# Half-tile instead of quarter-tile pieces of the mixing projections, between the steps of attention and delta rule, with another tile order

## The chip, the cores and the metric

One core of a Trainium2 chip runs the whole layer in one program. The metric is the device time of one execution in microseconds (us). The kernel before takes 1328.13 us, the median of 3 runs (1328.02 to 1328.16).

## The reference, cut to what matters

One decoder layer over 512 positions of width 1024, in fp32. The mixing half computes three branches from one normalised input `n`:

```python
n = rms_norm(h, ln_mix_pre)
da_q, da_k, da_v, dn_q, dn_k, dn_v, dn_z, dn_b, dn_a, ca_q, gate_logits = split(n @ w_in)
y_a = diff_attention(da_q, da_k, da_v, ...)        # 8 heads, two softmax maps a head
qkv = short_conv(concat(dn_q, dn_k, dn_v), conv_w) # causal, width 4, silu
o_dn = gated_delta_rule(cq, ck, cv, g, beta)       # 8 heads, chunks, a triangular solve in each
y_b = rms_norm(o_dn, dn_norm_g) * silu(dn_z)
mk, mv = split(rms_norm(mem, mem_norm_g) @ w_mem_kv)
y_c = memory_attention(ca_q, mk, mv)               # 4 heads, 256 memory tokens
proj = einsum('bsiw,iwd->bsid', stack(y_a, y_b, y_c), w_branch)
mixed = sum(sigmoid(gate_logits) * proj)
h = h + rms_norm(mixed @ w_out, ln_mix_post)
f = square(relu(rms_norm(h, ln_ff_pre) @ w_ff1)) @ w_ff2
h = h + rms_norm(f, ln_ff_post)
```

## The kernel before, in words

Every large product is cut into weight tiles of 1024 rows by 128 columns. A tile of weights is loaded by a DMA on SyncE's queue into `w_raw` (three buffers), split by ScalarE into a rounded part `w_hi` (L1105, "hi") and by VectorE into the rest `w_lo` (L1407, "lo"; three slots), and TensorE multiplies it in 8 slices of 128 rows, three products to a slice: `n_hi` by `w_hi` (L1906), `n_lo` by `w_hi` (L1907), `n_hi` by `w_lo` (L1908). Such a tile is 24 multiplications of 512 columns into one of two banks of `acc`; ScalarE empties the bank ("evac") before the tile after the next may begin.

The mixing stage has 104 such tiles: `dq`, `dk`, `dv`, `dz` for the delta rule, `aq`, `ak`, `av` for the differential attention, `mk`, `mv`, `cq` for the memory attention (`mk` and `mv` over 256 columns), and 24 `gate` tiles. Between pieces of these tiles stand the 178 steps of the two other chains of work: `attn` (for a memory head cs, ct, cv; for a head av, as0, as1, at, ap, ay) and `delta` (for each of 4 pairs of heads dk, dE, dq, dv, dL, T1, dA, the solve Za, Wb, Z5, W5, Zl, Wl, then dU, dW, the chunks sa, sb, and dO). A step is a few short products or transposes on TensorE (into `ps_a` or `ps_d`), whose result is worked on by ScalarE, VectorE or GpSimd before the next step of its chain may start. The names in the profile: `d_XB` is what Za leaves and Wb reads, `sums_lo` is what dE reads, `o_a` what ay reads.

The order of all this is fixed before the program is built. `ORDER` is a table of tile kinds; `mixing_tiles` makes the sequence of tiles of it. `plan_order` then places the work of each engine: it gives each piece a length and the pieces that it needs (a table `parts` says how a tile is divided for TensorE), and lets each engine take, of the families that are ready, the first in a list of ranks; on TensorE a step that is ready goes ahead of the next piece of a tile. Every engine then runs its list strictly in order, and waits on semaphores.

What follows the mixing stage is the branch stage: 24 tiles `br` multiply the branches' outputs by `w_branch`, first the 8 of the memory attention. Its first tile waits for each slice `k` of the branch apart:

```python
if r % KT == 0:
    k_wait = lambda k, b=b: pe.wait_ge(yl_ready, KT * b + k + 1)
```

The branch outputs were stored to HBM by their steps (`y_scratch`), since SBUF has no room for them. The eight slices of the first branch are read back in the family "pre": SyncE loads slice kk into `y_st[kk % 2]` (L977; from kk = 2 on when the slice two before is done with its buffer, `yl_ready` at kk - 1), VectorE rounds it to `y_hi` (L1684), GpSimd makes the rest `y_lo` (L1070) and counts `yl_ready`. These three stand in the engines' fixed lists too, between the last steps of the mixing stage. dO of the last pair (L2053) is transposed on TensorE, multiplied on VectorE by `zs` into `d_ET` (L1675), and stored by SyncE (L968); `zs` comes of the last two tiles, `dz6` and `dz7`, by ScalarE (`z_t`, L1201) and VectorE (L1544), one after the other.

Of the kernel before, what the change touches and what calls it, by code (L numbers as in the profile page):

```python
# [86 lines left out]


ORDER = [("first", 0), ("z", 0), ("mem", 0), ("cq", 0), ("cq", 1), ("cq", 2), ("cq", 3), ("conv", 1), ("head", 0),
         ("head", 1), ("gate", 1), ("conv", 2), ("head", 2), ("gate", 2), ("head", 3), ("z", 1), ("gate", 1),  # L90
         ("head", 4), ("gate", 2), ("z", 2), ("head", 5), ("conv", 3), ("head", 6), ("gate", 2), ("head", 7),
         ("gate", 13), ("z", 3)]

# [112 lines left out]
def plan_order(tiles, need_free, n_first):  # L208
# [5 lines left out]
    n_mix = len(tiles)  # L214
    conv = [t for t in range(n_mix) if tiles[t][0] in ("dq", "dk", "dv")]
    zt = [t for t in range(n_mix) if tiles[t][0] == "dz"]
    gate = [t for t in range(n_mix) if tiles[t][0] == "gate"]
    spill = [i for i, s in enumerate(attn) if s[0] in ("cv", "ay")]
    short = lambda t: tiles[t][0] in ("mk", "mv")
    finished = lambda t: tiles[t][0] in ("dq", "dk", "dv", "dz")  # L220
    parts = {t: ((0, 4), (4, 8)) if short(t) else ((0, 2), (2, 4), (4, 6), (6, 8)) for t in range(n_mix)}
    last = {t: ("PE", "main", t) + parts[t][-1] for t in range(n_mix)}
    busy, needs, queue = {}, {}, {}

# [162 lines left out]
def plan_tiles():  # L387

    tiles, need_free = mixing_tiles()
    n_mix = len(tiles)  # L390
    order, planned = first_order(tiles), plan_order(tiles, need_free, FIRST)
    for e in order:
        order[e] += planned[e]
    tiles = list(tiles)
    for i in (2, 0, 1):
        tiles += [("br", i * KT + m) for m in range(KT)]
    tiles += [("out", m) for m in range(KT)]
    for half in range(2):
        tiles += [("f1", half * 16 + f) for f in range(16)]
        tiles += [("f2", (2 * half + g) * KT + m) for g in range(2) for m in range(KT)]  # L400
    return tiles, n_mix, order, need_free
# [1989 lines left out]
```

## Time and profile before

| what | us |
|---|---|
| median of 3 runs | 1328.13 (1328.02 to 1328.16) |
| the profiled execution, its time | 1327.76 |
| its span, from the first to the last instruction | 1326.0 |
| TensorE busy in it | 1307.4 (99%) |
| VectorE, ScalarE, GpSimd busy | 758.0, 461.7, 187.6 |
| mixing stage, tiles with steps between them | about 77 to 788.5 of the span |
| first tile of the branch stage on TensorE | starts at 788.53 |

The share of busy time names the bound (TensorE), but its ends are modelled, so a busy engine may still lose some tenths of a microsecond at each change of work. Two things are read from the trace instead: the list of what TensorE waited for, and the distance from one matmul's start to the next one's. Matmuls of 512 columns that follow each other start every 0.23 us, so a larger distance is a loss at that place.

### The profile page before, as it was taken

The numbers are of one execution on the slowest core, as the hardware profiler recorded it, in microseconds if no ns is written. First come the engines' busy times: TensorE is split into PE (matmuls) and PEld (weight loads), VectorE is DVE, ScalarE is ACT, GpSimd is POOL, SyncE is SP. The second block draws the span as 40 slices with busy tenths as digits, with TensorE's granted clock in tenths as the row PEclk, the third lists the DMA queues.
The fourth block names the chain that finished last, engine by engine and source line by source line (L and its number), as shares of the span: only waits on it lengthen the run. The fifth ranks groups of instructions, "written<-read, shape, count | busy, mean of one in ns | idle before, by whom it ended". The sixth has DMA issues, their size and how long they took to land.

```text
span 1326.0 us, 23795 instructions
## 1 busy us (share of the span) xinstructions
PE 1307.4 (99%) x10193; PEld 1092.5 (82%) x10193; DVE 758.0 (57%) x1278; ACT 461.7 (35%) x765; POOL 187.6 (14%) x128
## 2 busy tenths in 40 slices
PE   9999999999999999999999999999999999999997
PEld 8879988787788887888878888888888888888886
DVE  6786335576576576577965354555576522355335
ACT  5343433444353444343534331112433212222220
POOL 1023000013000023000331412233012200022000
PEclk9999999999999999999999999999999999999999
DMA  5155413221212232212223537653504333323321
GB/s 218 60 177 171 129 48 111 80 84 62 81 65 80 82 101 90 64 58 101 83 89 97 161 111 231 209 162 130 220 33 127 95 113 98 91 96 98 108 64 64
DMA packets 62832, 144.03 MB, mean 109 GB/s; under 512 B 5072, under 2 KB 28168, under 8 KB 62728
## 3 DMA queue, kind: packets, MB, share of 16 engines
q1 hardware_dynamic: 62728, 142.51, 33.2%
q8 instruction: 81, 1.33, 0.4%
q14 instruction: 23, 0.19, 0.1%
HBM read 127.79 MB, written 16.27 MB: 109 GB/s over the span
## 4 chain that ended last, share of the span: by engine, by line
PE 89%; DVE 6%; issue 2%; ACT 1%; DMA 1%; POOL 0%; SPq 0%; DVEq 0%; ACTq 0%; POOLq 0%
PE acc L1906 17%; PE acc L1908 16%; PE acc L1907 16%; PE ps_a L1907 2%; PE ps_a L1906 2%; PE ps_a L1908 2%; PE ps_a L2015 2%; PE ps_d L2093 2%; PE ps_d L2223 2%; PE ps_a L2223 2%; PE ps_d L2224 2%; PE ps_a L2225 2%; PE ps_a L2224 2%; PE ps_d L2225 2%; DVE w_lo L1407 1%
## 5 line engine op out<-in xcount | busy, mean ns | idle before, releaser
L1407 DVE TENSOR_TENSOR w_lo<-w_raw,w_hi 128x1024 fp32r<-128x1024 f32 x170 | 233.0, 1371 | 208.2 <-ACT w_hi L1105 207.5
L1105 ACT CAST w_hi<-w_raw 128x1024 fp32r<-128x1024 f32 x170 | 178.1, 1048 | 406.5 <-PE acc L1908 331.6
L1906 PE MATMUL acc<-n_hi,w_hi 128*128 128x512 f32 x744 | 303.3, 408 | 1.2 <-ACT conv_x L1180 1.2
L1908 PE MATMUL acc<-n_hi,w_lo 128*128 128x512 f32 x744 | 290.7, 391 | 0.0
L1907 PE MATMUL acc<-n_lo,w_hi 128*128 128x512 f32 x744 | 290.2, 390 | 0.0
L1906 PEld LDWEIGHTS acc<-n_hi,w_hi 128*128 128x128 f32 x744 | 139.9, 188 | 30.8 <-issue 3.8
L1908 PEld LDWEIGHTS acc<-n_hi,w_lo 128*128 128x128 f32 x744 | 139.6, 188 | 30.3
L1907 PEld LDWEIGHTS acc<-n_lo,w_hi 128*128 128x128 f32 x744 | 140.1, 188 | 25.8 <-issue 0.7
L1093 POOL TENSOR_TENSOR h_lo<-sq,h_hi 128x512 fp32r<-128x512 f32 x32 | 41.5, 1296 | 269.6 <-DVE h_hi L1822 269.6
L1906 PE MATMUL acc<-y_hi,w_hi 128*128 128x512 f32 x192 | 74.8, 390 | 0.0
L1908 PE MATMUL acc<-y_hi,w_lo 128*128 128x512 f32 x192 | 74.7, 389 | 0.0
L1907 PE MATMUL acc<-y_lo,w_hi 128*128 128x512 f32 x192 | 74.7, 389 | 0.0
L1407 DVE TENSOR_TENSOR wx_lo<-w_raw,wx_hi 128x1024 fp32r<-128x1024 f32 x27 | 41.9, 1556 | 54.0 <-ACT wx_hi L1105 54.0
L1076 POOL TENSOR_SCALAR gate_st<-gate_st 128x512 f32<-128x512 f32 x24 | 26.3, 1095 | 309.4 <-ACT gate_st L1187 309.4
L1340 ACT ACTIVATE sq<-relu 128x512 f32<-128x512 f32 x32 | 20.2, 632 | 114.4 <-DVE relu L1820 114.4
L1523 DVE SCALAR_TENSOR_TENSOR conv_y<-conv_x,par,conv_y 128x512 f32<-128x512 f32 x72 | 57.2, 794 | 2.6
L1105 ACT CAST wx_hi<-w_raw 128x1024 fp32r<-128x1024 f32 x27 | 28.1, 1044 | 51.1 <-PE acc L2225 27.6
L1047 POOL TENSOR_TENSOR sums_hi<-cst,par 128x1024 fp32r<-128x1024 f32 x4 | 8.6, 2150 | 262.4 <-PE ps_d L2049 150.2
L1906 PEld LDWEIGHTS acc<-y_hi,w_hi 128*128 128x128 f32 x192 | 36.0, 188 | 7.7
L1908 PEld LDWEIGHTS acc<-y_hi,w_lo 128*128 128x128 f32 x192 | 36.0, 188 | 7.5
L1907 PEld LDWEIGHTS acc<-y_lo,w_hi 128*128 128x128 f32 x192 | 36.1, 188 | 7.3
L1229 ACT ACTIVATE p_a<-ps_a,smd 128x512 f32<-128x512 f32 (+3 forms) x64 | 32.9, 529 | 16.6 <-DVE smd L1571 16.5
(434 smaller groups left out, 2455.8 us busy)
## 6 DMA issues: line engine op xcount, KB each, us to landing
w_raw<-weights SPq DMA_DIRECT2D x200, 512.0 KB, 3.5
gate_scratch<-gate_st SPq DMA_DIRECT2D x24, 256.0 KB, 4.3
g_in<-gate_scratch SPq DMA_DIRECT2D x24, 256.0 KB, 3.9
y_raw<-y_scratch SPq DMA_DIRECT2D x16, 256.0 KB, 3.7
x_tok<-x SPq DMA_DIRECT2D x4, 512.0 KB, 5.3
y_scratch<-y_st SPq DMA_DIRECT2D x4, 512.0 KB, 2.7
y_scratch<-d_ET SPq DMA_DIRECT2D x4, 512.0 KB, 2.6
y_scratch<-y_st SPq DMA_DIRECT2D x8, 256.0 KB, 2.3
```

Source lines behind the costliest of these rows:

```text
L1093: nc.gpsimd.tensor_tensor(h_lo[:, f % 16], sq[:, f % 2], h_hi[:, f % 16].bitcast(F32), ALU.subtract).then_inc(hl_ok, 1)
L1105: nc.scalar.copy(hi_of_tile(t), w_raw[:, t % RAW]).then_inc(hi_ready, 1)
L1229: last = nc.scalar.activation(p_a[:, m, pack_of[q]:pack_of[q] + w], flat(ps_a[:])[:, col:col + w], ACT.Exp, bias=nbs[:, n:n + 1], scale=SC ...
L1407: V_.tensor_tensor(lo_of_tile(t), w_raw[:, t % RAW], hi_of_tile(t).bitcast(F32), ALU.subtract).then_inc(lo_ready, 1)
L1523: ins = V_.scalar_tensor_tensor(out=y, in0=conv_x[:, n % 2, j:j + S], scalar=par[:, col + j:col + j + 1], in1=y, op0=ALU.mult, op1=ALU.add)
L1906: mm(bank, wh, hi_of(k), start=start and k == 0, stop=False)
L1907: mm(bank, wh, lo_of(k), start=False, stop=False)
L1908: last = mm(bank, wl, hi_of(k), start=False, stop=stop and k == KT - 1)
L2015: last = mm(ps[:, col:col + (q + 1) * P], qkv_T[rows_m, h % 2, 0, q * P:(q + 1) * P], qkv_T[rows_m, h % 2, 1, 0:(q + 1) * P], start=True, ...
L2223: mm(to, high, wh, start=kb == 0, stop=False)
L2224: mm(to, low, wh, start=False, stop=False)
L2225: return mm(to, high, wl, start=False, stop=kb == 2 * KT - 1)
```

## The change

In `plan_order`, a full weight tile is divided for TensorE in two pieces of four slices in place of four pieces of two, as the short tiles were already. So the places at which a step can stand between pieces are half as many. And `ORDER` is another one: the tiles are the same, but `z` 1 and some gates come earlier, and fewer gates (9 in place of 13) stand between the last head and the last `z`. Nothing else is edited; the lists of all engines follow from the two.

```diff
-         ("head", 1), ("gate", 1), ("conv", 2), ("head", 2), ("gate", 2), ("head", 3), ("z", 1), ("gate", 1),
-         ("head", 4), ("gate", 2), ("z", 2), ("head", 5), ("conv", 3), ("head", 6), ("gate", 2), ("head", 7),
-         ("gate", 13), ("z", 3)]
+         ("head", 1), ("z", 1), ("gate", 1), ("conv", 2), ("head", 2), ("gate", 1), ("head", 3), ("head", 4),
+         ("z", 2), ("head", 5), ("gate", 3), ("conv", 3), ("gate", 3), ("head", 6), ("gate", 4), ("head", 7),
+         ("gate", 9), ("z", 3)]
...
-    parts = {t: ((0, 4), (4, 8)) if short(t) else ((0, 2), (2, 4), (4, 6), (6, 8)) for t in range(n_mix)}
+    parts = {t: ((0, 4), (4, 8)) if short(t) else ((0, 4), (4, 8)) for t in range(n_mix)}
```

**The end of the mixing stage on TensorE.** L1906 to L1908 with `n_` are slices of the last `dz` tiles, with `y_` the first branch tile, L2053 is dO of the last pair. Before:

```order
L1908 MATMUL acc<-n_hi,w_lo 128x512
L2053 MATMUL ps_d<-cst,d_LT 128x128 x8
L1906 MATMUL acc<-n_hi,w_hi 128x512
L1907 MATMUL acc<-n_lo,w_hi 128x512
L1908 MATMUL acc<-n_hi,w_lo 128x512
```

and now:

```order
L1908 MATMUL acc<-n_hi,w_lo 128x512
L2053 MATMUL ps_d<-cst,d_LT 128x128 x8
L1906 MATMUL acc<-y_hi,w_hi 128x512
L1907 MATMUL acc<-y_lo,w_hi 128x512
L1908 MATMUL acc<-y_hi,w_lo 128x512
```

dO stood ahead of the last quarter of `dz6` and all of `dz7`; now it stands behind both, right ahead of the branch stage.

**The end of the mixing stage on VectorE**, from the end of the last sb step (L1607) to the first branch tile's result (L1772). Before:

```order
L1607 TENSOR_TENSOR d_LT<-d_LT,smd 128x1024
L1407 TENSOR_TENSOR w_lo<-w_raw,w_hi 128x1024 x2
L1544 SCALAR_TENSOR_TENSOR zs<-z_t,zs 128x512
L1407 TENSOR_TENSOR w_lo<-w_raw,w_hi 128x1024
L1544 SCALAR_TENSOR_TENSOR zs<-z_t,zs 128x512
L1675 SCALAR_TENSOR_TENSOR d_ET<-ps_d,smd,zs 128x1024
L1772 TENSOR_TENSOR mix_acc<-acc,g_in 128x512
```

and now:

```order
L1607 TENSOR_TENSOR d_LT<-d_LT,smd 128x1024
L1407 TENSOR_TENSOR w_lo<-w_raw,w_hi 128x1024 x2
L1544 SCALAR_TENSOR_TENSOR zs<-z_t,zs 128x512
L1684 CAST y_hi<-y_st 128x512 x2
L1544 SCALAR_TENSOR_TENSOR zs<-z_t,zs 128x512
L1675 SCALAR_TENSOR_TENSOR d_ET<-ps_d,smd,zs 128x1024
L1684 CAST y_hi<-y_st 128x512 x2
L1772 TENSOR_TENSOR mix_acc<-acc,g_in 128x512
```

Of the eight roundings of the first branch (L1684) all stood ahead of L1607; now the last four stand behind it, two behind the first `zs` and two behind the last `d_ET`. The second `w_lo` of the pair is now that of the third branch tile, `br2`, which before stood between the two `zs`. On SyncE's queue the last reload (L977) now stands behind the store of that `d_ET` (L968).

**The second pair of the delta rule on VectorE**, after its dA step (L1639): L1642 into `d_XB` is the first Za, L1559 to L1571 the maximum of head 0's first scores. Before:

```order
L1639 TENSOR_TENSOR d_AT<-ps_d,d_ET 128x1024
L1640 TENSOR_TENSOR d_TT<-cst,d_XB 128x256
L1559 TENSOR_TENSOR strip<-strip,cst 128x8x128
L1563 TENSOR_TENSOR ps_a<-ps_a,strip 128x3x256
L1569 TENSOR_REDUCE smd<-ps_a 128x1 x3
L1571 TENSOR_SCALAR smd<-smd 128x3
L1407 TENSOR_TENSOR w_lo<-w_raw,w_hi 128x1024
L1642 TENSOR_TENSOR d_XB<-cst,ps_d 128x256
```

and now:

```order
L1639 TENSOR_TENSOR d_AT<-ps_d,d_ET 128x1024
L1640 TENSOR_TENSOR d_TT<-cst,d_XB 128x256
L1642 TENSOR_TENSOR d_XB<-cst,ps_d 128x256
L1407 TENSOR_TENSOR w_lo<-w_raw,w_hi 128x1024
L1559 TENSOR_TENSOR strip<-strip,cst 128x8x128
L1563 TENSOR_TENSOR ps_a<-ps_a,strip 128x3x256
L1569 TENSOR_REDUCE smd<-ps_a 128x1 x3
L1571 TENSOR_SCALAR smd<-smd 128x3
```

`d_XB` moved ahead of the maximum and of a weight split.

## Rows read from the trace of the kernel before

**Rows 1.** What TensorE waited for, 50 to 800 us: us in total, times, longest.

```profile
PE ps_d L2057 <- POOL sums_lo L1048: 1.4, 1, 1.4
...
PE ps_d L2069 <- DVE d_XB L1642: 1.2, 2, 0.7
PE ps_a L2030 <- DVE o_a L1599: 1.1, 1, 1.1
PE acc L1908 <- issue: 1.0, 1, 1.0
```

**Rows 2.** Timeline of TensorE at two waits: start us, us, instruction, [idle before <-releaser].

```profile
86.89 0.39 PE L1908 MATMUL acc<-n_hi,w_lo 128*128 128x512 f32 x1
88.71 0.47 PE L2057 MATMUL ps_d<-sums_hi,after_r 128*128 128x512 f32 x1 [1.43 <-POOL sums_lo L1048]
...
513.42 0.63 PE L2030 MATMUL ps_a<-cst,o_a 128*128 128x128 f32 x4 [1.15 <-DVE o_a L1599]
```

**Rows 3.** Timeline of TensorE, the joints of two pieces with steps at 304 us.

```profile
304.42 0.39 PE L1908 MATMUL acc<-n_hi,w_lo 128*128 128x512 f32 x1
304.74 0.75 PE L2065 MATMUL ps_d<-cst,d_XB 32*32 32x32 f32 x64
...
307.66 0.47 PE L1906 MATMUL acc<-n_hi,w_hi 128*128 128x512 f32 x1
307.98 0.39 PE L1907 MATMUL acc<-n_lo,w_hi 128*128 128x512 f32 x1
```

**Rows 4.** Timeline of VectorE: one instruction of step ap, at two places.

```profile
504.33 2.42 DVE L1595 TENSOR_TENSOR p_a<-o_a 128x512 f32<-128x512 f32 x1 [0.42 <-ACT o_a L1237]
...
675.10 0.69 DVE L1595 TENSOR_TENSOR p_a<-o_a 128x512 f32<-128x512 f32 x1 [0.30 <-ACT o_a L1237]
```

**Rows 5.** Timeline of TensorE at the end of the mixing stage.

```profile
780.83 1.03 PE L2053 MATMUL ps_d<-cst,d_LT 128*128 128x128 f32 x8
781.62 0.48 PE L1906 MATMUL acc<-n_hi,w_hi 128*128 128x512 f32 x1
...
788.53 0.39 PE L1906 MATMUL acc<-y_hi,w_hi 128*128 128x512 f32 x1
...
793.97 0.39 PE L1906 MATMUL acc<-y_hi,w_hi 128*128 128x512 f32 x1
```

**Rows 6.** Timelines of ScalarE and VectorE around the last `dz` tile.

```profile
788.79 1.05 ACT L1105 CAST w_hi<-w_raw 128x1024 fp32r<-128x1024 f32 x1 [3.18 <-PE acc L1908]
790.41 0.63 ACT L1201 ACTIVATE z_t<-zs 128x512 f32<-128x512 f32 x1
...
772.43 0.60 DVE L1661 SCALAR_TENSOR_TENSOR state<-state,e_all,ps_d 128x128 f32<-128x128 f32 x2
...
778.31 1.23 DVE L1607 TENSOR_TENSOR d_LT<-d_LT,smd 128x1024 f32<-128x1024 f32 x1
...
789.87 1.23 DVE L1407 TENSOR_TENSOR w_lo<-w_raw,w_hi 128x1024 fp32r<-128x1024 f32 x1 [3.54 <-ACT w_hi L1105]
791.08 0.69 DVE L1544 SCALAR_TENSOR_TENSOR zs<-z_t,zs 128x512 f32<-128x512 f32 x1
791.88 1.28 DVE L1675 SCALAR_TENSOR_TENSOR d_ET<-ps_d,smd,zs 128x1024 f32<-128x1024 f32 x1
```

**Rows 7.** One reload on SyncE's queue, VectorE and GpSimd; the last `y_lo`.

```profile
744.42 5.54 SPq L977 DMA_DIRECT2D y_st<-y_scratch  x3
...
747.83 0.43 DVE L1684 CAST y_hi<-y_st 128x512 fp32r<-128x512 f32 x1 [4.58 <-DMA y_st<-y_scratch]
...
748.33 1.28 POOL L1070 TENSOR_TENSOR y_lo<-y_st,y_hi 128x512 fp32r<-128x512 f32 x1 [2.71 <-DVE y_hi L1684]
...
766.71 1.29 POOL L1070 TENSOR_TENSOR y_lo<-y_st,y_hi 128x512 fp32r<-128x512 f32 x1 [0.97 <-DVE y_hi L1684]
```

**Rows 8.** The tile `y_st`: its DMAs from issue to landing.

```profile
DMA to landing us min/median/max: 2.0/2.8/4.9
```

**Rows 9.** Busy time of one stretch: PE, PEld, DVE, ACT, POOL, granted clock, DMA share, GB/s.

```profile
964.00:968.00 4.00, 2.80 (x23) 2.32 (x22) 3.59 (x16) 2.03 (x2) 0.00 (x0) 1.00 0.00 0
```

## The prediction

> **What bounds the kernel now.** I read the page first: TensorE is busy nearly all of the span and most of the chain of work is its own matmuls. So time can only be won where TensorE waits or loses a little at a change of work, and lost where a new wait appears. Then the list of what TensorE waited for: in the mixing stage three releasers other than its own issue count, `sums_lo`, `d_XB` (twice) and `o_a`, 3.7 us of shown idle [rows 1]. Last the timelines: start to start a wait costs a little more than its shown idle. From the last slice to dE is 1.82 us where two matmuls that follow each other stand 0.23 apart [rows 2], so 1.6 lost. In the same way I count 1.3 at `o_a` and 0.7 at each `d_XB`, 4.3 us in all. The four causes: GpSimd's `sums_lo` came late; Za's result stood behind a maximum and a weight split on VectorE; and VectorE itself was slow while GpSimd worked (the same instruction took 2.42 and 0.69 us [rows 4]).
>
> At the end of the stage nothing waits: the first branch tile follows `dz7` at 788.53 and takes 5.44 us, 0.68 a slice [rows 5]. It can, since the last of the eight `y_lo` was ready at 768 [rows 7], 20 us earlier.
>
> **The change part by part.**
>
> *Joints on TensorE.* The multiplications are the same. In the order I count 143 groups of steps between pieces before and 126 now; 17 groups were joined to a neighbour. A return to the tile costs 0.09 (0.32 from first to second matmul where 0.23 is usual), and leaving for a step of 32 rows as much [rows 3]; a joint of two steps costs between nothing and 0.2, by the distances at those in the trace. 17 times (-0.18 to 0.11) is -3 to 2 us; summed over the kinds of joint that the new order has, it is +0.5, which I take.
>
> *The four waits in the middle.* Of the first two `dz` tiles dk had 2 slices ahead of it and 10 between it and dE, and now has 4 and 12; so dE stands 4 slices (2.7 us) later, and 2 slices (1.36) later than dk. If `sums_lo` moves with dk, 1.6 becomes 0.25; if it doesn't, nothing is left. `d_XB` of the second pair now stands ahead of the maximum. For the other two I laid the new order's pieces out at 2.72 us a half tile and each step at its duration in the trace: the VectorE work of ap has 10.5 us of cover ahead of ay where it had 9.6, and Wb of the last pair 4.5 where it had 2.4. So of 4.3 us I take 4.0 as gained; ends: 1.5 (only dE) and 4.3, or 5.5 if one of the issue waits, the largest of which is 1.0 [rows 1], is gone too.
>
> *New waits in the middle.* The same layout shows every other step covered, but some by little: Za behind dA in pairs 1 to 3 by about 1 us, dO of pair 2 by 0.4. dA is where GpSimd works longest, and [rows 4] show what that can add on VectorE: 1.7 us to one instruction. I take 1.0 us in all; ends 0 and 4.
>
> *The end of the stage.* This is the large term. I count from T, the end of `dz7` on TensorE, 788.53 in the trace of before [rows 5].
> - VectorE's fifth rounding `y_hi` stands behind `w_lo` of `br2` and behind `zs` of `dz6`. `w_lo` of `br2` needs the slot of `dz7`, so its `w_hi` can't start before T: it started at T+0.26, `w_lo` at T+1.34, the next instruction at T+2.55 [rows 6]. So `zs` of `dz6` runs at T+2.55, and the fifth and sixth `y_hi` (0.43 each [rows 7]) from T+3.3 to T+4.1.
> - GpSimd's `y_lo` starts 0.07 after its `y_hi` and takes 1.3 [rows 7]: the fifth is ready at T+5.1, the sixth at T+6.4.
> - The seventh reload waits for the fifth `y_lo` (its buffer). From issue to the start of its rounding a reload took 3.4 us, 744.42 to 747.83 [rows 7]: rounding at T+8.5, `y_lo` ready at T+10.3.
> - The eighth stands on SyncE's queue behind the store of dO. `z_t` of `dz7` waits for `zs` of `dz6` (T+3.3 to T+3.9), then `zs`, then `d_ET` from T+4.8 to T+6.1 [durations in rows 6], store, reload issued at T+6.5, landed at T+9.9; its `y_lo` stands behind the seventh, ready at T+11.65.
> - TensorE: dO, 0.79 (780.83 to 781.62 [rows 5]), then from T+0.9 four slices until T+3.6. The fifth waits until T+5.1, the sixth until T+6.4, the seventh until T+10.3, the eighth until T+11.7, and ends at T+12.4. Without a wait the tile would end at T+6.3. So 6.1 us are lost, and nothing gives them back: the following tiles ran without a gap before. Behind the eighth reload SyncE's queue holds the loads of the first gates and of weights, which are first needed at the end of this tile or later.
>
> The ends of this term are those of the reload. 2.0 to 4.9 us from issue to landing [rows 8]; with 2.6 from issue to rounding it is 5.3, with 4.9 it is 7.6. dO itself shouldn't wait: the last sb ended on VectorE 7.1 us after its first instruction (772.43 to 779.54 [rows 6]), and 8.2 us of half tiles cover it.
>
> The Trainium skill, page "DMA: Bandwidth & Descriptors", section "Anatomy of one DMA", gives about 2.0 us fixed and the bytes at 436 GB/s, an estimate of 2.6 us for a slice of 256 KB. Our one row shows 3.4 to the rounding; by the page the sum would be 0.8 us less.
>
> **The sum.** 0.5 - 4.0 + 1.0 + 6.1 = +3.6 us. On the profiled execution's 1327.76 (its span is 1326.0, 1.76 less) that is 1331.4; on the median, which is 0.37 above, 1331.7.
>
> **The rivals.**
> - *The waits are all that counts, and the end is covered.* If the fifth to eighth `y_lo` were ready by T+3.6, T+4.3, T+5.0 and T+5.6, the tile would run as before and only the gain is left: 1328.1 - 4.0 + 0.5 + 1.0 at most, 1325.6, and 1324.1 without new waits and with the gain's upper end. Against it: `w_lo` of `br2` can't be earlier than `dz7`'s end, and VectorE keeps its order. It decides at the point where the fifth `y_lo` passes T+3.6; I have it 1.5 later, and the seventh 4 later. Chance 0.09.
> - *No change.* The stall is at its lower end, 5.3, no new wait comes and some issue waits go: 5.3 + 0.5 - 5.0 = +0.8, 1328.9. For it: the issue waits [rows 1] have no fixed place, and nothing in the layout must wait. Against it: all three have to fall the same way. Chance 0.34 (the layout's margins are about as large as its error).
> - *New waits in the middle at their upper end*, from VectorE slowed by GpSimd behind dA: +3 on my sum, 1334.7. It is a case of slower. Chance 0.12.
> - *The clock.* In the stall TensorE works about one part in two. A stretch with 1.2 us of idle in 4 kept the granted clock at 1.00, 2.4 GHz [rows 9]. If it fell to 1.2 GHz for half a tile, the matmuls there would take twice as long, 2.7 more: 1334.4. Chance 0.05. The Trainium skill, page "TensorE: Matmul & The Clock Gate", section "HAM oscillation", tells of matmuls that ran at half the clock after each wait for a DMA; no row of before has such a wait, and the price above is worked out without it.
> - *My forecast*, 1330.9 to 1333.5: chance 0.40.
>
> **How the numbers follow.** About 0.2% (2.7 us) is what a measurement of this kernel can tell from no change. Forecast, upper new waits and clock are slower, 0.57; no change 0.34; faster 0.09. The forecast lies 0.9 us from the bound, so slower and same are near to each other. The range leaves out the first rival and the sum of all upper ends: low is the no-change case less 1.6, 1327.3, high is 1331.7 with the stall at 7.6 and new waits at 4, 1336.2.
>
> **What would show it.** In the profile after: TensorE's list should have a wait for `y_lo` in the first branch tile (four gaps, near 1.5, 0.6, 3.2 and 0.7 us) and `sums_lo`, `d_XB` and `o_a` should be short or gone. `d_ET` should stand between the roundings, and the seventh reload be issued about 5 us behind `dz7`. Wrong would be: no gap ahead of a `y_hi` matmul; a gap that is larger than 8 us, which would be a reload chain that started late; or a sum of waits in the middle above 6 us.

## The result: 1335.23 us, and the profile after

The changed kernel takes 1335.23 us (median of 3 runs, 1332.50 to 1336.35), 1.0052 times the time before, 95% interval 1.0038 to 1.0065. Six more runs beside other kernels gave 1331.48 to 1337.67, median 1333.45, ratio 1.004 (1.0028 to 1.0053). So it is slower, by about 0.5%, and its runs are 4 to 6 us apart where those of before are 0.1 to 2.7.

From the page of the profiled execution (its time is the median itself): span, busy time of the engines, and of the DMA queues the one that carries instructions (packets, MB, share):

```profile
span 1333.4 us, 23795 instructions
...
PE 1311.4 (98%) x10193; PEld 1096.4 (82%) x10193; DVE 749.2 (56%) x1278; ACT 461.5 (35%) x765; POOL 184.8 (14%) x128
...
q8 instruction: 81, 1.33, 0.4%
```

The list of what TensorE waited for from 50 to 800 us (engine, line, what for, releaser: us in total, times, longest; "issue" is time in which the engine waited for nothing that the profile shows):

```profile
PE acc L1906 <- POOL y_lo L1070: 6.0, 4, 2.1
PE ps_d L2069 <- issue: 2.2, 2, 1.6
PE acc L1906 <- DVE w_lo L1407: 1.6, 1, 1.6
PE acc L1906 <- ACT conv_x L1180: 1.2, 1, 1.2
...
```

Against [rows 1], `sums_lo`, `d_XB` and `o_a` are gone. In their place stand four waits for `y_lo` and one for a `w_lo`. The engine's own issue has about the same sum as before, 2.6 against 2.5, but with one wait of 1.6 where the longest was 1.0; its three lines that [rows 1] leave out are, before:

```profile
PE ps_d L2069 <- issue: 0.7, 2, 0.5
PE ps_d L2071 <- issue: 0.6, 1, 0.6
PE ps_d L2065 <- issue: 0.2, 1, 0.2
```

The end of the stage on TensorE, which answers to [rows 5] (start, us, engine, line, operation; idle before and releaser in brackets):

```profile
785.40 1.03 PE L2053 MATMUL ps_d<-cst,d_LT 128*128 128x128 f32 x8
786.19 0.47 PE L1906 MATMUL acc<-y_hi,w_hi 128*128 128x512 f32 x1
790.41 0.50 PE L1906 MATMUL acc<-y_hi,w_hi 128*128 128x512 f32 x1 [1.21 <-POOL y_lo L1070]
792.09 0.50 PE L1906 MATMUL acc<-y_hi,w_hi 128*128 128x512 f32 x1 [0.72 <-POOL y_lo L1070]
794.96 0.50 PE L1906 MATMUL acc<-y_hi,w_hi 128*128 128x512 f32 x1 [1.91 <-POOL y_lo L1070]
798.06 0.80 PE L1906 MATMUL acc<-y_hi,w_hi 128*128 128x512 f32 x1 [2.13 <-POOL y_lo L1070]
798.65 0.63 PE L1907 MATMUL acc<-y_lo,w_hi 128*128 128x512 f32 x1
799.08 0.63 PE L1908 MATMUL acc<-y_hi,w_lo 128*128 128x512 f32 x1
803.67 0.39 PE L1907 MATMUL acc<-y_lo,w_hi 128*128 128x512 f32 x1
803.90 0.40 PE L1908 MATMUL acc<-y_hi,w_lo 128*128 128x512 f32 x1
```

dO is at 785.40 (T of the prediction), and the four gaps stand ahead of the fifth to eighth slice. Behind the last gap two matmuls that follow each other start 0.43 us apart (798.65 and 799.08); at 803.67 it is 0.23 again. The stretches show why; the stretch of [rows 9] was less idle, and its clock stood at 1.00 (stretch, length, busy us of PE, PEld, DVE, ACT, POOL with counts, then the granted clock, DMA share, GB/s):

```profile
786.00:790.00 4.00, 3.20 (x16) 2.35 (x14) 3.24 (x5) 1.82 (x3) 1.02 (x1) 1.00 0.01 4
790.00:794.00 4.00, 1.93 (x6) 0.97 (x6) 2.61 (x3) 0.00 (x0) 2.39 (x3) 1.00 0.47 158
794.00:798.00 4.00, 0.97 (x3) 0.48 (x3) 0.43 (x1) 0.00 (x0) 2.16 (x2) 0.84 0.94 286
798.00:802.00 4.00, 3.94 (x9) 3.17 (x10) 1.81 (x2) 1.04 (x1) 0.01 (x1) 0.50 0.81 269
802.00:806.00 4.00, 4.00 (x16) 3.18 (x15) 0.53 (x2) 0.00 (x0) 1.28 (x1) 0.81 0.68 233
```

TensorE was busy 1.93 us of 4, then 0.97 of 4; then the granted clock stood at 0.50, the 1.2 GHz level, for some 5 us in which it worked without a pause.

One table holds the time of every kernel by stretch, from the starts of matmuls in each profiled execution (us). The first column ends at the first matmul of the last `mv` slice, the second at the last matmul of `dz7`, the third is what the first `y_hi` matmul comes later than the usual 0.23 behind that one, and the last is the first three branch tiles. Behind them all kernels run alike, 513.2 to 513.5:

| kernel | to the last `mv` slice | to the end of `dz7` | from there to the first `y_hi` matmul | three branch tiles |
|---|---|---|---|---|
| before | 155.4 | 632.8 | 0.0 | 16.3 |
| after | 157.3 | 627.8 | 0.8 | 26.1 |
| again (after, another run) | 160.0 | 627.9 | 0.8 | 25.8 |
| filled | 160.7 | 628.5 | 0.8 | 23.4 |
| shift_after | 154.7 | 627.6 | 0.8 | 26.0 |
| shift_filled | 154.8 | 628.2 | 0.8 | 23.4 |
| six_buffers | 155.5 | 627.8 | 3.8 | 17.5 |
| tail | 155.7 | 628.2 | 0.8 | 17.5 |
| tail_shift | 154.4 | 627.7 | 0.8 | 17.4 |
| early_split | 153.4 | 628.5 | 0.8 | 17.3 |
| halves_old_order | 156.1 | 625.3 | 16.2 | 20.8 |
| quarters_new_order | 155.6 | 654.5 | 0.0 | 19.4 |
| shift_before | 159.8 | 635.7 | 0.0 | 16.3 |
| shift_before_96 | 162.8 | 636.5 | 0.0 | 16.3 |

After against before: +1.9, -5.0, +0.8 (dO, which stood inside the second stretch before) and +9.8, together +7.5. The second stretch gained what was hoped for and more; the branch tiles lost twice that; and the stretch up to the end of the memory tiles, where the prediction had 1.35 to gain at dE, lost 1.9 here and 4.6 in the second execution.

### The profile page after: what moved, and what is told of

Its sections match the earlier page's. It is cut to its first block, busy times and chain, and to the rows that moved or that the text cites. A ratio compares the mean times of both kernels' runs of the same rounds, so it can differ in the third digit from the quotient of the medians.

```text
span 1333.4 us, 23795 instructions
## 1 busy us (share of the span) xinstructions
PE 1311.4 (98%) x10193; PEld 1096.4 (82%) x10193; DVE 749.2 (56%) x1278; ACT 461.5 (35%) x765; POOL 184.8 (14%) x128
## 3 DMA queue, kind: packets, MB, share of 16 engines
q8 instruction: 81, 1.33, 0.4%
## 4 chain that ended last, share of the span: by engine, by line
PE 94%; DVE 2%; ACT 1%; DMA 1%; issue 1%; SPq 0%; POOL 0%; DVEq 0%; ACTq 0%
PE acc L1906 18%; PE acc L1908 18%; PE acc L1907 18%; PE ps_d L2093 2%; PE ps_a L1908 2%; PE ps_a L1907 2%; PE ps_a L1906 2%; PE ps_a L2015 2%; PE ps_d L2224 2%; PE ps_a L2224 2%; PE ps_d L2225 2%; PE ps_a L2225 2%; PE ps_a L2223 2%; PE ps_d L2223 2%; PE ps_a L2026 1%; PE acc L2224 1%
## 5 line engine op out<-in xcount | busy, mean ns | idle before, releaser
L1407 DVE TENSOR_TENSOR w_lo<-w_raw,w_hi 128x1024 fp32r<-128x1024 f32 x170 | 225.8, 1329 | 192.2 <-ACT w_hi L1105 191.0
L1906 PE MATMUL acc<-n_hi,w_hi 128*128 128x512 f32 x744 | 301.8, 406 | 1.2 <-ACT conv_x L1180 1.2
L1908 PE MATMUL acc<-n_hi,w_lo 128*128 128x512 f32 x744 | 290.6, 391 | 0.0
L1906 PEld LDWEIGHTS acc<-n_hi,w_hi 128*128 128x128 f32 x744 | 139.9, 188 | 32.4 <-issue 4.8
L1908 PEld LDWEIGHTS acc<-n_hi,w_lo 128*128 128x128 f32 x744 | 139.7, 188 | 30.2
L1906 PE MATMUL acc<-y_hi,w_hi 128*128 128x512 f32 x192 | 76.5, 399 | 6.0 <-POOL y_lo L1070 6.0
L1908 PE MATMUL acc<-y_hi,w_lo 128*128 128x512 f32 x192 | 75.8, 395 | 0.0
L1906 PEld LDWEIGHTS acc<-y_hi,w_hi 128*128 128x128 f32 x192 | 36.7, 191 | 15.3 <-POOL y_lo L1070 7.7
L1908 PEld LDWEIGHTS acc<-y_hi,w_lo 128*128 128x128 f32 x192 | 36.6, 191 | 7.8
L1906 PE MATMUL acc<-m_hi,w_hi 128*128 128x256 f32 x128 | 38.1, 298 | 1.6 <-DVE w_lo L1407 1.6
```

The source lines that it names most:

```text
L1407: V_.tensor_tensor(lo_of_tile(t), w_raw[:, t % RAW], hi_of_tile(t).bitcast(F32), ALU.subtract).then_inc(lo_ready, 1)
L1906: mm(bank, wh, hi_of(k), start=start and k == 0, stop=False)
L1908: last = mm(bank, wl, hi_of(k), start=False, stop=stop and k == KT - 1)
```

## The experiments

**The end of the stage: wait, clock and their parts**

*again.* The changed kernel unaltered.

> The changed kernel once more, beside the others on one chip. Theory A (the stall at the first branch tile costs 7 us of waits, and a granted TensorE clock that falls to one half behind it costs 2.8 more): the profile again has four gaps ahead of y_hi matmuls in the first branch tile of about 1.2, 0.7, 1.9 and 2.1 us, and matmuls that start 0.43 us apart instead of 0.23 behind the last one; time 1332 to 1337 us. Theory B (the clock fell by chance in that one execution): gaps as before, the matmuls behind them 0.23 apart, time near 1332.

1333.45 us median; the profiled run was the slowest of the six, 1337.67. The four gaps are there (the list below ends at 800 us and has three of them; the fourth, 1.38, ends at 800.76), and the clock falls again, in this run already ahead of the last gap (0.68 from 794 to 798), so it is not chance (theory A). What is larger than in the first profile is the issue wait in the memory tiles:

```profile
PE ps_d L2069 <- issue: 3.9, 2, 2.3
PE acc L1906 <- POOL y_lo L1070: 3.6, 3, 1.7
```

*filled.* Matmuls into an unused bank, ahead of each slice's wait in the first branch tile; their results are not used:

```diff
-                        k_wait = lambda k, b=b: pe.wait_ge(yl_ready, KT * b + k + 1)
+                        def k_wait(k, b=b, r=r, t0=t0):
+                            if r == 0:
...
+                                for _ in range((0, 0, 0, 0, 5, 3, 8, 9)[k]):
+                                    mm(ps_a[:, 0], hi_of_tile(t0)[:, 0], y_hi[0][:, 0], start=True, stop=True)
+                            pe.wait_ge(yl_ready, KT * b + k + 1)
```

> The changed kernel with 5, 3, 8 and 9 matmuls of 512 columns into an unused PSUM bank ahead of the last four slices of the first branch tile, 0.23 us each, so that TensorE works while it waits there. Nothing else is moved. Theory A: the waits stay, since the reloads come as late as before, but the granted clock stays at 1.00, so the twelve matmuls behind the last gap start 0.23 apart: 2.8 us less than the changed kernel where that one loses its clock there, 1332.4. Rival (the slow matmuls there have another cause than TensorE's idling, such as the transfers beside them): they stay 0.43 apart, no change in time, 1335.

1334.11 us (1329.86 to 1336.61): no gain in the median, and 1336.61 for the profiled run. But its branch tiles took 23.4 instead of 26.1, with the clock at 1.00 throughout; here are its stretches over the last two gaps and behind them:

```profile
798.00:802.00 4.00, 3.92 (x17) 2.71 (x15) 0.43 (x1) 0.00 (x0) 2.35 (x2) 1.00 0.99 316
802.00:806.00 4.00, 4.00 (x18) 3.30 (x18) 1.92 (x2) 1.05 (x1) 0.00 (x0) 1.00 0.82 272
```

The transfers beside it are as busy as in the first profile (0.99), so they are not what slows the matmuls; TensorE's idling is. The gain was covered by the memory tiles, 160.7 to their end instead of 157.3. That sent us there.

*shift_filled.* The same on a stream with less of those issue waits (below), to be held against `shift_after`.

> The changed kernel with 96 more instructions and the 25 matmuls that fill its stall, to be held against the one with 96 more alone (1332.35), since the issue waits hid the gain in the run before. Theory A: the granted clock stays at 1.00 behind the stall, 2.4 to 2.8 us less: 1329.7. Rival: no change, 1332.

1329.70 us (1329.10 to 1331.90) against 1332.35 of `shift_after`: 2.65 less, the branch tiles 23.4 against 26.0. So the clock costs 2.6 us, and the pure waits 7.1 (23.4 less 16.3). Before took 1327.96 beside the first and 1328.12 beside the second.

*six_buffers.* Reloads in six buffers instead of two. By the second line the planner also places the roundings anew, all eight ahead of the last `w_lo` and `zs` on VectorE; no run changes one of the two without the other:

```diff
+            return (y_st, conv_y, conv_x)[kk % 6 // 2][:, kk % 2, 0:S]
...
-        deps = [...] if kk < 2 else [("POOL", "pre", kk - 2)]
+        deps = [...] if kk < 6 else [("POOL", "pre", kk - 6)]
...
```

> Reloads of the first branch go to six buffers (y_st, and the two halves of conv_y and conv_x, which are free by then) instead of two, so that they need not wait for one another, and all eight roundings stand ahead of the last w_lo and zs on VectorE; TensorE's order is the same. Theory A: the stall and the clock loss behind it are gone, 9.8 us less than the changed kernel's profiled run: 1325.4 us, 2.7 below the kernel before. Rival (the stall has another cause, such as dO or the weights of the second and third branch tile, and takes a new place): a wait of some us in the first two branch tiles, 1329 or more.

1327.67 us (1324.94 to 1330.85), ratio 0.9991 (0.9982 to 1.0). The `y_lo` waits are gone, and half of the rival came true: a new wait stands at dO,

```profile
785.97 1.68 PE L2059 MATMUL ps_d<-cst,d_LT 128*128 128x128 f32 x8 [2.31 <-DVE d_LT L1613]
787.29 0.78 PE L1912 MATMUL acc<-y_hi,w_hi 128*128 128x512 f32 x1
787.87 0.63 PE L1913 MATMUL acc<-y_lo,w_hi 128*128 128x512 f32 x1
```

and the clock falls behind that wait too (matmuls of 0.63 us, as behind the stall). VectorE's last sb step was late, by the roundings ahead of it and by two instructions of 128x8 that took seven times their usual 0.17 us:

```profile
780.36 1.14 DVE L1611 SCALAR_TENSOR_TENSOR smd<-smd,sml 128x8 f32<-128x8 f32 x1
781.53 1.22 DVE L1394 TENSOR_SCALAR smd<-smd 128x8 int32<-128x8 int32 x1
782.78 0.17 DVE L1395 TENSOR_SCALAR smd<-smd 128x8 int32<-128x8 int32 x1
```

GpSimd made two `y_lo` in just that time:

```profile
780.18 2.54 POOL L1076 TENSOR_TENSOR y_lo<-y_st,y_hi 128x512 fp32r<-128x512 f32 x2
```

*tail.* Six buffers too, and the last four roundings behind the sb step:

```diff
+    late = [("pre", kk) for kk in range(4, KT)]
+    dve[:] = [s for s in dve if s not in late]
+    at = max(i for i, s in enumerate(dve) if s[0] == "delta" and delta_steps()[s[1]][0] == "sb") + 1
+    dve[at:at] = late
```

> Six reload buffers as in the run before, but on VectorE the last four roundings stand behind the last sb step and ahead of the w_lo of the second branch tile, not ahead of that sb step. Theory A (the 3.0 us ahead of dO in the run with six buffers are VectorE's sb step, pushed back by four roundings and by GpSimd beside it): dO follows dz7 at once, no wait for y_lo, clock 1.00: 4 us less than with six buffers alone, 1323.5. Rival (the last y_lo are now late): waits of 1 to 3 us for y_lo, 1325 to 1327.

1326.42 us (1325.37 to 1330.30), ratio 0.9989 (0.9980 to 0.9997). dO follows `dz7` at once, the branch tiles take 17.5, 1.2 above the kernel before (0.3 us for the last `y_lo`, 0.3 for `mix_acc`; the other 0.6 stays open). Where theory A looked it holds: that wait and the clock loss are gone, and the rival's 1 to 3 us for `y_lo` are 0.3. The time is 2.9 above what was expected and in the rival's range, but 2.0 us of issue waits are again in the memory tiles. The runs of `six_buffers` and `tail` overlap, so the gain of one over the other is read from the profiles.

**The two parts of the change alone**

*halves_old_order*: half pieces, with the `ORDER` of before.

> Half-tile pieces alone, with the tile order of before. By the planner's own lists the delta rule then ends 18 us behind the last weight tile and the last y_lo 27 us behind it, so theory A (the end is what half pieces cost, since the steps are spread over more tiles) expects 20 to 27 us lost at the first branch tile, with the clock: 1346 to 1353. Rival (the new tile order makes the stall, not the pieces): 1326 to 1330.

*quarters_new_order*: the new `ORDER`, with quarter pieces.

> The new tile order alone, with quarter-tile pieces. By the planner's own lists TensorE then stands idle for 17 us at the second half of the stage (at dE of the last pair and at the fifth head's at and ap) and the last y_lo comes 8 us behind the last tile. Theory A (either part alone is bad, the two fit together but for the end): 1343 to 1350. Rival (the new order is good by itself, and half pieces are what costs): 1326 to 1330.

1339.89 us (two runs, 1338.21 and 1341.56; ratio 1.0087, 1.0070 to 1.0105) and 1351.49 (1350.27 and 1352.71; 1.0177, 1.0158 to 1.0195). Either is worse than both together. The half pieces push the steps back, so dO waits at the end (halves_old_order):

```profile
PE ps_d L2053 <- DVE d_LT L1607: 7.3, 1, 7.3
```

The place is the expected one, and so is the loss there: 16.2 ahead of the first `y_hi` matmul and 4.5 in the branch tiles, 20.7 of the 20 to 27. The whole is only 11.8 above the kernel before, since the stage ahead of it was 7.5 shorter: steps of it moved to its end. The new order with quarter pieces lets TensorE stand in the second half of the stage (quarters_new_order):

```profile
PE ps_a L2021 <- DVE p_a L1591: 9.0, 1, 9.0
PE ps_d L2057 <- POOL sums_lo L1048: 6.4, 2, 4.9
```

So each part alone is worse than the two together; only at the end they don't fit.

**The issue waits**

In all profiles the waits over 0.5 us that are put down to "issue" in these stretches begin at an instruction of TensorE whose number, counted in the trace, leaves 193 when divided by 256: numbers 1985, 2497, 3009, 3521, 6849, 9921, 13505 and 13761. They end 1.2 to 1.6 us behind the end of a transfer of the instruction queue. The page counts 81 such transfers of together 1.33 MB, 16.4 KB each; TensorE has 20770 instruction records, 256.4 for each transfer. In the first profile of after the longest stands in a Wb step, whose 64 small matmuls (128 records) started within about 1 us up to the wait:

```profile
141.79 0.23 PE L2069 MATMUL ps_d<-d_TT,d_XB 32*32 32x32 f32 x4
143.59 0.18 PE L2069 MATMUL ps_d<-d_TT,d_XB 32*32 32x32 f32 x1 [1.57 <-issue]
```

and the clock falls behind it, to 0.60 over a stretch in which TensorE works all the time:

```profile
140.00:144.00 4.00, 2.43 (x137) 2.14 (x136) 1.30 (x2) 0.93 (x3) 0.00 (x0) 1.00 0.48 152
144.00:148.00 4.00, 4.00 (x23) 4.00 (x23) 1.22 (x2) 1.61 (x3) 0.00 (x0) 0.60 0.21 80
```

The edit that tests it moves all later instructions by some places and touches nothing else:

```diff
                     mm(acc[:, 0, 0:P], ones[:], ones[:], start=True, stop=True)
+                    for _ in range(3):
+                        pe.wait_ge(ones_set, 1)
```

The expectations speak of 96 more instructions for three waits. It was 48 in every one of these kernels: the traces hold 20818 records, with two waits as with three. So `shift_before` and `shift_before_96` have the same stream, and the second is a repeat.

*shift_after*, the changed kernel with three waits:

> The changed kernel with three waits on a semaphore that has long been set behind each of the 48 matmuls ahead of the first rows, which puts 96 more instructions into TensorE's stream there and moves all later ones by 96; no other engine and no order is touched. Theory F (TensorE's instructions come in blocks of 256 by DMA, and a wait put down to issue is a block that comes late; in the profiles so far all such waits over 0.5 us begin at instruction numbers that leave 193 when divided by 256, and end 1.2 to 1.6 us behind a transfer of that queue): with 96 more, no two blocks end inside neighbouring Wb and Za steps, so the waits in the memory tiles (together 2.6 to 4.3 us in three profiles) and the fall of the granted clock behind them (1 to 2 us) go; the stall at the first branch tile stays. 1330 to 1331 us, with a spread under 2 us. Rival (the issue waits belong to the Wb steps themselves, whatever the place in the stream): no change, 1332 to 1337.

*shift_before*, the kernel before with two:

> The kernel before with two such waits behind each of the 48 early matmuls: 48 more instructions in TensorE's stream. A layout of its instructions with a wait wherever 256 of them are used up in under 4 us gives 5 us of such waits at the place where they stand and 10 with 48 more, at other steps. Theory F: new issue waits at instruction numbers that leave 193 when divided by 256, 2 to 5 us slower than before: 1330 to 1333. Rival (the place in the stream is of no account): 1328.

*shift_before_96*, the kernel before with three:

> The kernel before with 96 more instructions early in TensorE's stream. The same layout as for 48 more gives 1.9 us of issue waits where it gives 5 without. Theory F: 1 to 3 us faster than the kernel before, 1325 to 1327, so that the two tile orders, each with its instruction blocks out of the way, are to be compared with this and not with 1328.1. Rival: 1328 or slower.

`shift_after`: 1332.35 us, with runs from 1332.26 to 1333.61 (1.4 apart instead of 4 to 6); issue waits 0.7 us in all, the clock falls only in the stall. That is 1 to 2 us more than expected (the stall still costs 9.7), and by the time alone it would pass for the rival's 1332 to 1337; what tells the two apart is the profile, in which the waits are gone. `shift_before`: 1336.29 us (1334.97 to 1337.09), ratio 1.0063 (1.0048 to 1.0078); the repeat 1336.22 (1333.99 to 1338.84), 1.0063 (1.0049 to 1.0076). 8 us for 48 idle instructions, more than the 2 to 5 expected, because the clock falls behind two of the waits (0.72 from 124 to 128 us, 0.63 from 528 to 532). From the list for `shift_before`:

```profile
PE ps_d L2071 <- issue: 3.7, 3, 2.6
PE acc L1909 <- issue: 2.6, 1, 2.6
```

Its waits begin at 1985, 2497, 3521, 6849 and 9921: other steps than before, but again a remainder of 193. So the place in the stream decides, not the step. The 1325 to 1327 expected of `shift_before_96` were for a stream that was not built; the kernel before with its blocks out of the way was not run.

**Both repairs**

*tail_shift* is `tail` with the 48 instructions.

> Both: six buffers with the late roundings, and 96 more instructions early in TensorE's stream. If theories A and F both hold, nothing is left of the stall, of the issue waits or of the lost clock: 1320.5 to 1322, 6 to 7 below the kernel before. If only A holds: 1323.5.

1324.24 us (1323.64 to 1325.11), ratio 0.9971 (0.9959 to 0.9982): faster than before and after. The expected 1320.5 to 1322 counted 96. Its list:

```profile
PE acc L1919 <- DVE w_lo L1418: 1.6, 1, 1.6
...
PE ps_d L2084 <- issue: 0.4, 1, 0.4
PE acc L1919 <- POOL y_lo L1081: 0.3, 1, 0.3
```

*early_split* is `tail_shift` with one more edit. The 1.6 us for `w_lo` stand where [rows 2] had dE's wait. In after dE runs at once and the first memory tile waits:

```profile
90.27 0.39 PE L2057 MATMUL ps_d<-sums_lo,after_r 128*128 128x512 f32 x1
92.27 0.38 PE L1906 MATMUL acc<-m_hi,w_hi 128*128 128x256 f32 x1 [1.60 <-DVE w_lo L1407]
```

VectorE has that `w_lo` behind the whole of dk, which ended at 91.0. So the split was put ahead of dk:

```diff
+    for e, split in (("ACT", ("hi", mk)), ("DVE", ("lo", mk))):
+        order[e].remove(split)
+        order[e].insert(next(i for i, s in enumerate(order[e]) if s[0] == "delta"), split)
```

> The run with six buffers, late roundings and 96 more instructions, and in it the first memory tile's w_hi on ScalarE and w_lo on VectorE stand ahead of their dk steps instead of behind them. In the profile after, dE no longer waits for sums_lo, but the first memory tile waits 1.6 us for this w_lo, behind the 5 us of dk on VectorE. Theory G (that gain was given back there, by the order on VectorE): the wait goes, 1.6 us less than the run without it, 1322.6. Rival (dk, now 1 us later, holds up dE, dq or GpSimd instead): another wait of 1 us or more within the next 15 us, 1323.5 to 1324.5.

1323.26 us (1322.80 to 1323.48), ratio 0.9964 (0.9950 to 0.9977), 1.0 below `tail_shift` where 1.6 was expected. The wait is gone, but dv now waits for ScalarE's part of dq, so theory and rival are both half right:

```profile
PE ps_d L2066 <- ACT d_U L1266: 1.3, 1, 1.3
```

It is the fastest version of this study, 4.7 us below the kernel before.

## Why the prediction was right in sign and short in size

Forecast 1331.7, measured 1335.23 (and 1333.45): slower, as said, inside the range, but the first above the forecast's own span of 1330.9 to 1333.5 and the second at its edge. In the profiled executions 3.6 were forecast and 7.5 came. Nearly all of the miss lies at the end, where 6.1 were forecast and 9.8 came: 1.0 more wait, and 2.7 of lost clock. The joints, the middle waits and the new waits make -2.5 together; the rest of the table makes -2.3. That this agrees is luck, as the first three points show. Some luck is in the range too: its upper end holds a longer stall and more new waits, and no lost clock.

- *Joints, +0.5.* No loss of that size shows. From the memory tiles to dO the stage is 5.0 shorter, 4.2 without dO's 0.8. Counted from start to start, less the usual distance, the waits for other engines and for issue in it came to 5.0 us before and to 0.7 now. So nothing is left as a loss at the joints; they may have won some tenths, since one step of 32 small matmuls more stands in this stretch than before.
- *The four middle waits, -4.0.* `d_XB` and `o_a` went as said, and with them issue waits in the same stretch that were not counted. dE's 1.6 is the mis-sized part: it went from dE to the next tile's `w_lo`, 1.60. The step asked when `sums_lo` is ready, and not what else VectorE still owed at that place.
- *New waits, +1.0.* Not at Za or dO, where they were put. There are the `w_lo` and 2.2 of issue waits with 1.5 of lost clock, in the memory tiles, whose pieces the change doesn't touch. The list of before had 2.5 us of issue waits [rows 1], and the prediction left them as having no fixed place. They come at certain instruction numbers only, though not at each of them in every run.
- *The stall, +6.1.* The mechanism was right but for one step, and the pure wait is 7.1. The eighth `y_lo` was to stand behind the seventh; it waited for its own reload. The four slices were said to start at T+5.1, 6.4, 10.3 and 11.7; they did at 5.0, 6.7, 9.6 and 12.7. The timelines of VectorE and GpSimd show what was mis-sized:

```profile
787.88 0.69 DVE L1544 SCALAR_TENSOR_TENSOR zs<-z_t,zs 128x512 f32<-128x512 f32 x1
788.48 0.75 DVE L1684 CAST y_hi<-y_st 128x512 fp32r<-128x512 f32 x2
788.98 3.06 POOL L1070 TENSOR_TENSOR y_lo<-y_st,y_hi 128x512 fp32r<-128x512 f32 x2 [10.24 <-DVE y_hi L1684]
789.26 1.64 DVE L1544 SCALAR_TENSOR_TENSOR zs<-z_t,zs 128x512 f32<-128x512 f32 x1
791.02 1.28 DVE L1675 SCALAR_TENSOR_TENSOR d_ET<-ps_d,smd,zs 128x1024 f32<-128x1024 f32 x1
793.14 0.43 DVE L1684 CAST y_hi<-y_st 128x512 fp32r<-128x512 f32 x1 [0.84 <-DMA y_st<-y_scratch]
796.24 0.43 DVE L1684 CAST y_hi<-y_st 128x512 fp32r<-128x512 f32 x1 [2.67 <-DMA y_st<-y_scratch]
```

The second `zs` took 1.64 instead of 0.69, beside GpSimd's `y_lo`. The prediction knew this [rows 4] and used it for the middle only. So `d_ET` ended at T+6.9, not 6.1, and on SyncE's queue its store and the eighth reload behind it were late by as much:

```profile
792.33 0.32 SPq L968 DMA_DIRECT2D y_scratch<-d_ET  x1
792.69 0.43 SPq L977 DMA_DIRECT2D y_st<-y_scratch  x1
```

From there it took 3.55 to the rounding (3.4 by [rows 7]). The seventh reload was faster, 2.8 from its issue at 790.38. The section of the Trainium skill that the prediction quotes for 2.6 ("DMA: Bandwidth & Descriptors", "Anatomy of one DMA") is about transfers that GpSimd issues; SyncE issued these. And the 2.0 and 4.9 of [rows 8] are those of stores of `y_st`: the eight reloads of before took 2.6 to 3.7 from issue to landing, so the ends of this term had another source than it says.
- *The clock.* Its price was right: 2.7 said, 2.6 measured. Its chance, 0.05, is the step that failed. It rested on a stretch with 1.2 us idle in 4 [rows 9]; the forecast's own gaps of 3.2 and 0.7 around a slice of 0.7 made a stretch with TensorE idle for most of the time, for which no row of before spoke. "About one part in two" was misread too: by its own times TensorE worked 2.7 us of the 8.8 from T+3.6 to T+12.4. That rival's 1334.4 is 0.8 below the result; the 1334.7 of the rival with more new waits is nearer, but what it priced, VectorE slowed behind dA, did not come. The section "HAM oscillation" of the Trainium skill's page "TensorE: Matmul & The Clock Gate", which the prediction names there, tells of matmuls at half the clock behind each wait for a DMA, and here the trace agrees: 0.50 behind the waits for a reload, the longest 2.13 us.
- *No change* fell because the stall was not at its lower end (7.1 and the clock, in place of 5.3) and the first stretch lost 1.9, so that the middle won 2.3 in all and not 4.5.

## What to carry to other kernels

A plan that moves the end of a chain must be read to the first consumer behind the stage: here 5 us won in 630 were lost twice over at one tile, where a double buffer and a fixed queue had lost their lead. Where TensorE idles for most of a stall, count it twice: once as wait (7.1 us here), once as matmuls at the lower clock behind it (2.6). And where an order is searched on a planner's model, look whether bursts of small instructions meet the ends of instruction blocks; here 48 idle instructions far ahead moved the time of one order by 8 us, more than the change of order did.

## What the runs showed of the hardware that was not expected

- TensorE's instructions arrive in blocks of 256 (256.4 records to a transfer), and a block that comes late stopped it for 0.5 to 3.0 us, always at the same remainder. The Trainium skill, "Runtime: NRT & Kernel Launch", section "Instruction fetch mechanics", has blocks of 16 KiB or 256 instructions, with the crossing mostly hidden. The 16.4 KB agree; hidden it was not at the numbers above, all behind 256 records that were used up in 1.2 to 4.8 us. But not every such block came late: in `again` the 256 records ahead of number 14785 took 1.2 us, and no wait followed. The transfer ahead of number 1985 began at 118.9 us in the first profile of after and at 122.4 in `again`, which has the wait of 2.3 us there; why, and whether this makes the spread between runs, is not shown.
- VectorE instructions of 0.17 us took 1.14 and 1.22 in `six_buffers` while GpSimd worked, and ended when GpSimd's did (781.50 and 782.75 us; GpSimd 781.48 and 782.72). "SBUF — State Buffer" of the Trainium skill, section "SBUF: two separate sides", tells of a pair of ports that GpSimd and some kinds of VectorE instructions share, and that one of the two holds for a whole instruction while the other stands. The times of these rows agree, as does the `zs` of 1.64; whether both small instructions are of such a kind, no run here shows.
- The granted clock fell behind a single issue wait of 1.57 us among the memory tiles (0.60 over 4 us) in after, and not behind one of the same length in halves_old_order (1.58 us, clock 1.00); what tells the two apart was not tried.
